# Gain rows of the second block written to DRAM by DMA from SBUF columns, without turning them on TensorE first

## The reference, cut to what matters

```python
def first_block(x, ...):
    for l in range(DEPTH):                       # DEPTH = 2
        x = x + 0.5 * swiglu(rms_norm(x, ffn1_norm[l]), ...)
        ...                                      # mixer
        x = x + 0.5 * swiglu(rms_norm(x, ffn2_norm[l]), ...)
    return rms_norm(x, final_norm)

def second_block(...):
    for layer in range(DEPTH):
        sh_m, sc_m, gt_m, sh_f, sc_f, gt_f = ada_chunks(c, w_ada[layer], b_ada[layer])
        csh_m, csc_m, cgt_m, csh_f, csc_f, cgt_f = ada_chunks(c_ctx, w_ada[layer], b_ada[layer])
        ...
        h = h + gt_m * rms_norm_2(y, g_post_m)
        f = conv_ffn(modulate(h, g_pre_f, sh_f, sc_f), ...)
        h = h + gt_f * rms_norm_2(f, g_post_f)
        if with_ctx:                             # layer 0 only
            hc = hc + cgt_m * rms_norm_2(yc, g_post_m)
            ...
            hc = hc + cgt_f * rms_norm_2(fc, g_post_f)
    return h
```

## Time and profile before

| | |
|---|---|
| median of 3 executions | 1949.35 us |
| the profiled execution | 1949.95 us |
| its span, from the first to the last instruction | 1948.1 us |
| outside the span | 1.85 us |
| PE busy | 98% of the span |
| DVE busy | 65% |
| ACT busy | 47% |
| DMA engines, mean | 166 GB/s |

### The profile page before, as it was taken

One profiled execution on the slowest core, in us unless ns is written; L12 is line 12 of the kernel. 1 busy time (PEld: TensorE's weight loads), 2 busy tenths in 40 slices (PEclk: granted clock), 3 DMA queues, 4 the chain that ended last, 5 costly groups with the idle time before them and its releaser, 6 DMA issues.

```text
span 1948.1 us, 28728 instructions
## 1 busy us (share of the span) xinstructions
PE 1903.9 (98%) x11974; PEld 1625.2 (83%) x11974; DVE 1267.7 (65%) x1658; ACT 917.9 (47%) x1290; POOL 13.9 (1%) x17
## 2 busy tenths in 40 slices
PE   7999999999999999999999999999999999979998
PEld 6888969888888888788889878988888889679997
DVE  5776796766576668776765464765554367757774
ACT  5334565334533455653464355633342355655553
POOL 0000000000000000000000110000000000000000
PEclk9999999999999999999999999999999999999999
DMA  7776426766476643676453221222222223024452
GB/s 280 281 279 216 180 106 224 285 251 229 153 264 250 242 160 121 247 275 260 161 191 114 108 77 66 97 99 99 106 87 108 87 87 112 31 87 171 176 194 87
DMA packets 50960, 323.79 MB, mean 166 GB/s; under 512 B 5472, under 2 KB 9744, under 8 KB 12816
## 3 DMA queue, kind: packets, MB, share of 16 engines
q1 hardware_dynamic: 39024, 270.09, 38.3%
q10 hardware_dynamic: 11808, 51.86, 7.0%
HBM read 320.86 MB, written 1.07 MB: 165 GB/s over the span
## 4 chain that ended last, share of the span: by engine, by line
PE 92%; DVE 4%; ACT 2%; issue 1%; DMA 0%; ACTq 0%; DVEq 0%
PE ps L535 89%; PE ps L867 1%; DVE s_big L2189 1%; DVE s_wl L1898 1%; ACT s_wh L1227 0%; PE ps L728 0%; PE ps L705 0%; ACT s_big L1397 0%; DVE s_tmp L2411 0%; DVE s_X L2387 0%; PE ps L829 0%; DVE s_X L2084 0%; DMA s_X<-in_x 0%; DVE ps L2122 0%; DVE s_st L2128 0%
## 5 line engine op out<-in xcount | busy, mean ns | idle before, releaser
L535 PE MATMUL ps<-s_xx,s_wh 128*128 128x512 f32 (+1 forms) x3328 | 899.0, 348 | 11.6 <-DVE s_wl L1968 10.4
L1898 DVE TENSOR_TENSOR s_wl<-s_raw,s_wh 128x2048 fp32r<-128x2048 f32 x213 | 488.3, 2294 | 292.3 <-ACT s_wh L1227 292.2
L535 PE MATMUL ps<-s_xx,s_wl 128*128 128x256 f32 (+1 forms) x2208 | 669.2, 303 | 0.6 <-DVE s_xx L2414 0.6
L535 PEld LDWEIGHTS ps<-s_xx,s_wh 128*128 128x128 f32 x3328 | 579.3, 190 | 106.2 <-DVE s_wl L1968 10.7
L1227 ACT ACTIVATE s_wh<-s_raw 128x2048 fp32r<-128x2048 f32 x213 | 404.8, 1907 | 133.2 <-PE ps L535 129.9
L535 PEld LDWEIGHTS ps<-s_xx,s_wl 128*128 128x128 f32 x2208 | 419.1, 190 | 19.3 <-issue 2.7
L535 PE MATMUL ps<-s_wh,s_hl 128*128 128x512 f32 (+1 forms) x608 | 232.0, 382 | 0.5 <-DVE s_hl L1990 0.5
L535 PE MATMUL ps<-s_wh,s_hh 128*128 128x512 f32 (+1 forms) x608 | 230.0, 378 | 0.0
L535 PE MATMUL ps<-s_wl,s_hh 128*128 128x512 f32 (+1 forms) x608 | 229.9, 378 | 0.0
L535 PE MATMUL ps<-s_wh,s_xx 128*128 128x256 f32 x928 | 178.9, 286 | 0.0
L1341 ACT ACTIVATE s_tmp<-s_tmp 128x512 f32<-128x512 f32 x44 | 27.8, 632 | 281.2 <-DVE s_tmp L2015 274.5
(11 more groups left out here) (228 smaller groups left out, 1653.4 us busy)
## 6 DMA issues: line engine op xcount, KB each, us to landing
s_big<-in_w_ada ACTq DMA_DIRECT2D x46, 1024.0 KB, 5.9
s_raw<-in_ffn_down SPq DMA_DIRECT2D x44, 1024.0 KB, 4.8
s_raw<-in_w_up SPq DMA_DIRECT2D x44, 1024.0 KB, 4.7
s_raw<-in_ffn_gate SPq DMA_DIRECT2D x43, 1024.0 KB, 4.9
s_raw<-in_ffn_up SPq DMA_DIRECT2D x43, 1024.0 KB, 4.8
s_raw<-in_w_down SPq DMA_DIRECT2D x22, 1024.0 KB, 4.7
s_raw<-in_w_in SPq DMA_DIRECT2D x18, 1024.0 KB, 4.7
s_raw<-in_w_in_ab SPq DMA_DIRECT2D x10, 1024.0 KB, 4.8
```

What stands on the lines that cost most here:

```text
L535: return pe.matmul(o, lhsT, rhs, start=start, stop=stop, skip_group_check=True)
L1898: dve.tensor_tensor(wide(wl, u), raw[:, u % SLOTS, :].rearrange("p (k n) -> p k n", k=8), f32(wide(wh, u)), SUB).then_inc(*w_low.tick(u))
```

## The change

The transposes on PE, the copies on ACT and the four DMAs of whole rows go. In their place the columns are written to DRAM as they stand: each of six DMAs takes 128 partitions with 8 numbers each and puts every single number (4 bytes) at its own address, 128 k + p. `final_norm` is written in the first stage of the program (`final_written`, in step j = 2 of the first feed-forward stage), the other five at n = 7 of the last one (`gains_written`). The DRAM tensor is now one row of 1024 numbers for each gain, so that reading back half a gain is 2048 bytes in one piece for each partition, where it was four pieces of 512 bytes for the gains that were interleaved in pairs. The read of `final_norm` waits for its own write alone, the others for `gains_out`, which counts the five.

```diff
-        gain_dram = nc.dram_tensor("gain_dram", [4, 16, 128], F).ap()
+        gain_dram = nc.dram_tensor("gain_dram", [6, 1024], F).ap()
...
         def gain_halves(key):
...
+            rows = gain_rows[key]
+            return [(rows[h], gain_dram[gain_at[key]:gain_at[key] + 1, 512 * h:512 * h + 512].to_broadcast([128, 512]))
+                    for h in range(2)]
...
-            def gain_lines_():
-
-                claim(4)
-                pe.wait_ge(*modulated[0])
-                pe.wait_ge(*modulated[1])
-                for i, (l, c) in enumerate(((0, 16), (0, 40))):
-                    pe.transpose(ps[4][0:16, 128 * i:128 * i + 128], mod[:, l, c:c + 8, :].rearrange("p k s -> p (k s)"),
-                                 const("ident"))
-                pe.transpose(ps[4][0:8, 256:384], mod[:, 1, 16:24, 0], const("ident"))
-                pe.transpose(ps[4][0:8, 384:512], v("final_norm", 0, 8), const("ident")).then_inc(*product.tick("gain lines"))
-                freed[4] = gains_copied[256]
...
-                    ffn("ffn2", l, None, {2: lambda: (stat(C, 3, 5, summed[C]), gain_lines_()), 3: lambda: spread(C, 4, 6, normed[C, 3]),
+                    ffn("ffn2", l, None, {2: lambda: stat(C, 3, 5, summed[C]), 3: lambda: spread(C, 4, 6, normed[C, 3]),
...
-            def gain_lines_out():
-                for n, at in ((16, slice(0, 256)), (8, slice(256, 512))):
-                    act.wait_ge(*product["gain lines"])
-                    act.activation(gain_lines[0:n, at], ps[4][0:n, at], ACT.Copy).then_inc(*gains_copied.tick(at.start))
-                act.wait_ge(*gains_copied[256])
-                for i, n in ((0, 16), (1, 16), (2, 8), (3, 8)):
-                    act.dma_start(gain_dram[i, 0:n, :], gain_lines[0:n, 128 * i:128 * i + 128]).then_inc(*gains_out.tick(0))
+            def final_written():
+                act.wait_ge(*vec_in[0])
+                act.dma_start(gain_dram[0:1, :].rearrange("o (k p) -> p (o k)", p=128), v("final_norm", 0, 8),
+                              allow_slow_non_contiguous=True).then_inc(
+                    *final_out.tick(0))
+
+            def gains_written():
+
+                act.wait_ge(*modulated[0])
+                act.wait_ge(*modulated[1])
+                for key in (("m", 0, 0), ("m", 0, 1), ("f", 0, 0), ("f", 0, 1), ("m", 1, 0)):
+                    c, at = {"m": 16, "f": 40}[key[0]], gain_at[key]
+                    act.dma_start(gain_dram[at:at + 1, :].rearrange("o (k p) -> p (o k)", p=128),
+                                  mod[:, key[1], c:c + 8, key[2]], allow_slow_non_contiguous=True).then_inc(*gains_out.tick(0))
 
             def gains(key, free):
 
                 act.wait_ge(*free)
-                act.wait_ge(*gains_out[0])
+                act.wait_ge(*(final_out if key == "final" else gains_out)[0])
...
-            ffn("ffn1", 0, {4: lambda: sines(1), 7: lambda: sines(0)})
+            ffn("ffn1", 0, {2: final_written, 4: lambda: sines(1), 7: lambda: sines(0)})
...
-            ffn("ffn2", 1, {}, {1: ctx_squares, 2: lambda: (ctx_root(), gain_lines_out())} | {
+            ffn("ffn2", 1, {}, {1: ctx_squares, 2: ctx_root} | {
                 p + 3: lambda p=p: ctx_spread(p) for p in range(4)} | {
-                    8: lambda: (gains("final", x_low[("pre", 0, 1), 3]), ctx_tokens(0), ctx_tokens(1)),
+                    7: gains_written, 8: lambda: (gains("final", x_low[("pre", 0, 1), 3]), ctx_tokens(0), ctx_tokens(1)),
```

More of the change, by code:

```diff
@@ L146, in program @@
         bias_in = [signal(f"bias_in{i}", 16) for i in range(4)]
-        gains_out, gains_copied = signal("gains_out", 16), signal("gains_copied")
+        final_out, gains_out = signal("final_out", 16), signal("gains_out", 16)
         gain_in = {key: signal("gain_in_" + "".join(map(str, key)), 16) for key in
@@ L317, in program @@
                      ("m", 1, 0): (aux[:, 0, :], aux[:, 1, :])}
-        gain_lines = aux[0:16, 0, :]
+        gain_at = {"final": 0, ("m", 0, 0): 1, ("m", 0, 1): 2, ("f", 0, 0): 3, ("f", 0, 1): 4, ("m", 1, 0): 5}
         def gain_halves(key):
[L321 to L325, removed]
+            rows = gain_rows[key]
+            return [(rows[h], gain_dram[gain_at[key]:gain_at[key] + 1, 512 * h:512 * h + 512].to_broadcast([128, 512]))
+                    for h in range(2)]
         turn_bank = {("pre", 0, 0): (4, 5, 6, 7), ("m", 0, 0): (0, 2, 3, 4), ("m", 0, 1): (0, 3, 4, 7),
```

## The result

The changed kernel takes 1967.07 us, the median of 4 runs (1966.16 to 1970.78); the kernel before takes 1949.4 us beside it. The ratio is 1.0095, 95% interval [1.0078, 1.0112]: slower by 17.7 us, less than 1%, but far outside the spread of the runs. "No change" was forecast, with a range to 1951.7. The profiled execution took 1968.68 us with a span of 1966.8, 18.7 longer than before.

What follows compares the result with a forecast made beforehand. PE, busy 98% of the span, was taken to bound the kernel. The only nonzero term, -0.46 us for the transposes, took the profiled 1949.95 to 1949.49; less 0.60 to reach a median, 1948.9 us, range 1947.5 to 1951.7.

Steps and rivals of the forecast that it cites:

- No change: Whole kernel: forecast 1948.9 us, a change of 0.02% that can't be told from none; chance of same 0.86.
- The bound: Whole kernel: PE, busy 98% of the span, sets the time; an edit pays only through PE's instructions or waits.
- The transposes, -0.46 us: PE at n = 2: removing four transposes saves 0.46 us, lower end 0.36, and what follows moves along.
- Rival (1): Behind the hand-over at 978.96 us, ACT, DVE, a load or semaphore keeps the 0.46 us from arriving; 1949.35 us, chance 0.17.
- The copies and issues at n = 2, 0: ACT at n = 2: removing copies and four DMA issues gains 0, since they end before ACT is needed.
- The write of `final_norm`, 0: First stage: one more DMA issue on ACT costs 0, covered by 8.45 us of idle time; the write is small.
- The five issues, 0 with an upper end of 2.1: ACT at n = 7: five medians, 2.2 us, delay step 9's rounding without cost; the longest issues would cost 2.1 us.
- Rival (3): ACT at n = 7: each issue waits for the previous DMA's packets, rounding 8.8 us past its limit; 1957.7 us, chance 0.06.
- The five transfers, 0: DMA at n = 7: 320 packets per engine take 3.7 to 8.6 us; `final_norm` still arrives 9 us early, cost 0.
- which the loads' own lead should take: Weight loads near n = 7: at 27 ns a packet engine room is 3 us short, absorbed by their lead over ACT.
- Rival (2): 4-byte writes are much dearer, so the `final_norm` read lands after 1028.83 us and PE waits 7.7; 1956.6 us, chance 0.06.
- The rule that was set aside: Skill page on DMA: accesses strided in the last dimension become one descriptor per element; below 512 bytes, read-modify-write.

Runs made afterwards that it cites:

- e7: Changed kernel with the five writes moved from n = 7 to quieter stretches: two at about 1073 us, two at 1119, one at 1166; 1953.03 us, ratio 1.0017.
- e1: Changed kernel with all six writes as 128 whole pieces each instead of 1024 single numbers, gains read back in another order; 1948.86 us, ratio 0.9995.
- e8: Changed kernel with the five writes moved from n = 7: two at about 1073 us, three at 1119; 1949.02 us, ratio 1.0.
- e9: Kernel before plus five DMAs of 1024 single numbers at n = 7, from SBUF into SBUF, 8 bytes apart; 1949.73 us, ratio 1.0007.
- e6: Kernel before plus five writes of 1024 single numbers at n = 7 into spare DRAM, 512 bytes apart; 1954.83 us, ratio 1.0037.
- e2: Kernel before plus five writes of 1024 single numbers at n = 7 into spare DRAM, 64 bytes apart; 1954.19 us, ratio 1.0024.
- e3: Changed kernel with one of the five writes left as single numbers, the other four as 128 whole pieces; 1957.16 us, ratio 1.0044.
- e4: Kernel before plus only five writes of 1024 single numbers, side by side, at n = 7 into spare DRAM nobody reads; 1970.91 us, ratio 1.0109.

## Why the prediction was wrong, by its own steps

**The bound.** Right: PE sets the time, and the loss is made of waits of PE and of the low clock behind them.

**The transposes, -0.46 us.** About right, and at the lower end that was given, 0.36. In the changed kernel the next product starts 976.58 - 975.77 = 0.81 us after the sums do, and in the kernel before 975.86 - 974.70 = 1.16; the timelines of PE of both, the changed one first:

```profile
975.77 0.95 PE L533 MATMUL ps<-s_ca,s_tmp 128*128 128x2 f32 x8
976.58 0.49 PE L533 MATMUL ps<-s_wh,s_hl 128*128 128x512 f32 x1
```

```profile
974.70 0.95 PE L535 MATMUL ps<-s_ca,s_tmp 128*128 128x2 f32 x8
```

So 0.35 us are won, and DVE's units of weights, 1.08 us late against before at 805 us, are 0.75 late at 981, 0.33 less. In e7, which is free of the loss up to there, they are 0.42 ahead at 981. Rival (1), that it doesn't arrive, is not borne out this far; beyond, it can't be told: e1 and e8 have the gain in them and lie 0.4 us below the kernel before, less than the runs spread.

**The copies and issues at n = 2, 0.** Right: nothing waits there.

**The write of `final_norm`, 0.** Right in time, wrong in its reason. The issue stands ahead of the two roundings, at 42.42, and not in the idle time behind them that the prediction took as its cover; at 0.39 us this cost nothing. "The write is small" was the other reason; its landing took 12.6 us, and a load of `ffn_up` behind it kept ACT waiting (the line of the write, then ACT's timeline):

```profile
L1546 ACTq DMA_DIRECT2D gain_dram<-s_vec x1: 390/390/390, 42.4 to 42.4; - x1
...
DMA to landing us min/median/max: 12.6/12.6/12.6
```

```profile
59.98 1.92 ACT L1213 ACTIVATE s_wh<-s_raw 128x2048 fp32r<-128x2048 f32 x1 [2.62 <-DMA s_raw<-in_ffn_up]
```

PE didn't wait: its timeline from 40 to 70 us has no idle time. This was luck, not the cover that the prediction named.

**The five issues, 0 with an upper end of 2.1.** The issues are 0.38, 0.61 and 3.33 for three, 4.3 us in all, where five medians were 2.2; they end at 1011.97, within the limit of 1012.9. They cost nothing, as forecast. But the reads behind them took 6.56 us to issue where the earlier trace rows had at most 1.46 for one, and PE waited 3.4 us for what is behind those, inside the delay of the load. Rival (3) had this mechanism, for the writes, at 8.8 us; e1 and e9 show that it is not the issues as such.

**The five transfers, 0.** This is the step that failed, in two places: put at 0, it came to the whole 17.7 us. The first is the price. It was taken from the earlier trace rows, 11.6 to 27 ns a packet, and so 3.7 to 8.6 us for the five. The packets that those rows hold go into SBUF, or into DRAM in pieces of 512 bytes; e9 shows that for single numbers into SBUF the price is right: 16.2% of 33 us are 5.3 us, less 1.9 us for the reads the earlier trace rows; that leaves 3.4 us for 320 packets in each engine, 11 ns. For single numbers side by side in DRAM the same working gives, in the changed kernel, 61.6% of 33 us less 1.9 = 18.4 us, some 58 ns. And even that isn't the price: two writes with no other traffic show 8.6 ns a packet and take 11 us to land (e7). The second is the sentence "which the loads' own lead should take". The lead was never read from a row. The load in question is issued when DVE is done with a unit, at 1009.60 + 2.29 = 1011.89, and ACT rounds it from 1020.43 in the kernel before:

```profile
1020.43 1.92 ACT L1227 ACTIVATE s_wh<-s_raw 128x2048 fp32r<-128x2048 f32 x1 [1.75 <-PE ps L535]
```

So it has 8.5 us, and with its usual 4.8 us a room of 3.7. PE allows little more: DVE's unit ends at 1022.38 + 2.29 = 1024.67, in the chain after PE follows 0.75 us behind that, and it started at 1025.62 before, so 0.2 us. Three runs in which PE waits for this load alone bear that out:

| run | the load, us | PE's wait, us | difference |
|---|---|---|---|
| e6 | 12.28 | 3.48 | 8.80 |
| e2 | 12.66 | 3.80 | 8.86 |
| e3 | 15.53 | 6.72 | 8.81 |

Less the usual 4.8, the whole room is 4.0 us, as 3.7 + 0.2 says within 0.1. In e3 the load is 10.7 us longer than usual, as long as the one write takes to land (10.8). It goes through 4.0 us of room at once, which is why e3 costs 8 us and not a fifth of the loss: 6.7 us of wait, and the rest is the low clock behind it (0.50 in 1032 to 1036 us, 0.65 in the next 4). In the changed kernel the load takes 26.45 us; less 8.8 that is 17.6, the waits of PE.

**Rival (2).** It had the mechanism and the right sign with a chance of 0.06, and named the wrong waiter: the read of `final_norm`. That read lands at about 1041 us, 12 us after its old use, and yet no engine waits for it, for the weight load, which PE needs first, has by then moved that use to 1047.53. Hence 17.7 us and not 7.7. (With the load in time, the read would have held the norm by itself, by some 11 us: an estimate, 1041 less 1028.83 and the 0.75 us that the execution was late.) The forecast weighed the transfer by the reader of its own data and by the room in the engines; the dear thing was what stood behind it in every queue.

**The rule that was set aside.** The Trainium skill's "DMA: Bandwidth & Descriptors", section "Rules for kernel authors", was set against the rows of packets and given up for them. The trace now bears it out for DRAM: as separate elements the five writes cost 17.7 us, as whole pieces (e1) nothing. For SBUF (e9) the packets are as many, but they cost nothing that can be measured. The same page of the Trainium skill, in its section "Specifications", puts the read-modify-write at all transfers below 512 bytes; here pieces of 64 bytes land in 2.5 us and single numbers 64 bytes apart in 6.2, against 20.3 side by side, so that below 512 bytes it matters much how near small writes lie to each other. That the neighbours' read-modify-writes wait for one another would fit this, and is argued, not shown.

## What to carry to other kernels

A write to DRAM of single numbers side by side is priced by its landing, about 11 us for 1024 of them, and by every transfer issued within that time, on ACT's queue and on SP's; not by its bytes, its packets or its own reader. Send what a partition has side by side, or turn it on PE first as the kernel before does (0.4 us); if it can't be helped, put it where no transfer is needed before it has landed (11 us for one, 19 for three in a row). Where a row for an operation is missing, a row of another kind of target is no bound for it: the lead of the next load must be read and set against the worst case.

## What the runs showed of the hardware

- 1024 numbers of 4 bytes into DRAM, side by side: 10.8 to 13.1 us to land, alone or as one of two; three in a row up to 19.2 (e8), five up to 25.2, and 27.9 in e4. Into SBUF: 3.2 us (e9). As 128 pieces of 64 bytes: 2.5 us (e1).
- While such a write drains, other transfers stand still: a load of 1 MB takes 26.5 us instead of 4.8, with 1 GB/s moved by all engines for 8 us, while the engines can show as busy (share 2.08, with other transfers waiting) or as idle (e7, nothing waiting).
- ACT's issue of the next DMAs is held too: 6.56 us for two reads instead of the 0.82 in e8. Behind one such write (e3) it is 0.81.
- TensorE's granted clock was 0.50 (1.2 GHz) in 1036 to 1040 us, with PE idle since 1030.4, and 1.00 again in 1048 to 1052; this cost some 1.3 us beside the wait.
